# Dense gate and up of a two-layer transformer block with the weights as the stationary operand

## The reference

```python
def swiglu(h, wg, wu, wd):
    return (jax.nn.silu(h @ wg) * (h @ wu)) @ wd

for layer in range(DEPTH):
    h = h + hybrid_mixer(rms_norm(h, attn_norm[layer]), ...)
    hn = rms_norm(h, ffn_norm[layer])
    if layer % 2 == 0:
        h = h + swiglu(hn, dense_w_gate[j], dense_w_up[j], dense_w_down[j])
    else:
        h = h + moe_ffn(hn, moe_router[j], moe_w_gate[j], ...)
return rms_norm(h, final_norm)
```

## Time and profile before

| | before |
|---|---|
| median of 3 runs | 1602.93 us (1602.86 to 1602.99) |
| profiled execution, its own time | 1598.53 us |
| its span, first to last instruction | 1596.7 us |
| mean granted TensorE clock | 0.971 |
| TensorE matmuls busy | 1550.6 us (97%), 7086 of them |
| weight loads busy | 1252.5 us (78%) |
| DVE, ACT busy | 1266.9 us (79%), 1039.3 us (65%) |

### The profile page before, as it was taken

The page is one execution under the profiler, slowest core; times in us unless marked ns, Lnnn a source line. Parts: engine busy times, 40 slices in busy tenths (PEclk is TensorE's granted clock), DMA queues, the critical chain, the costliest instruction groups (busy, mean ns, idle before and its releaser), DMA issues.

```text
span 1596.7 us, 18779 instructions
## 1 busy us (share of the span) xinstructions
PE 1550.6 (97%) x7086; PEld 1252.5 (78%) x7086; DVE 1266.9 (79%) x1564; ACT 1039.3 (65%) x1328; POOL 58.7 (4%) x128
## 2 busy tenths in 40 slices
PE   7989999999899989999999999999999999999996
PEld 6867788888787778888888888888888888888885
DVE  6477655555548769899899899899899889999995
ACT  5444544443446457787788787787778778778774
POOL 2210000000113000000000000000000000000000
PEclk9978999999998789999999999999999999999998
DMA  7503454554252119999999999999999999999992
GB/s 282 191 2 106 177 197 172 182 187 160 86 180 106 54 67 372 373 359 360 341 358 365 334 357 370 343 354 368 337 364 356 343 358 362 345 369 362 358 359 95
DMA packets 181821, 431.61 MB, mean 270 GB/s; under 512 B 3808, under 2 KB 10336, under 8 KB 181728
## 3 DMA queue, kind: packets, MB, share of 16 engines
q1 hardware_dynamic: 180720, 428.01, 73.4%
q10 hardware_dynamic: 1008, 2.36, 0.4%
HBM read 429.31 MB, written 1.05 MB: 270 GB/s over the span
## 4 chain that ended last, share of the span: by engine, by line
PE 93%; DVE 4%; ACT 1%; issue 1%; POOL 0%; DMA 0%; DVEq 0%; SPq 0%; POOLq 0%
PE pair L828 50%; PE work L828 32%; PE pair L893 3%; PE work L804 2%; PE pair L804 2%; PE work L966 1%; PE work L815 1%; PE work L1069 1%; DVE arena L1519 0%; PE work L1083 0%; PE work L1084 0%; DMA h<-in_x 0%; DVE arena L1536 0%; DVE nmax L1550 0%; PE pair L896 0%
## 5 line engine op out<-in xcount | busy, mean ns | idle before, releaser
L1460 DVE TENSOR_TENSOR w_lo<-ring,w_hi 128x1024 fp32r<-128x1024 f32 (+3 forms) x810 | 967.1, 1215 | 198.5 <-ACT w_hi L1166 184.5
L1166 ACT ACTIVATE w_hi<-ring 128x1024 fp32r<-128x1024 f32 (+3 forms) x810 | 846.1, 1055 | 332.6 <-PE pair L828 177.2
L828 PE MATMUL pair<-w_hi,hnT_hi 128*128 128x512 f32 x672 | 269.2, 401 | 2.9 <-DVE hnT_lo L1468 2.6
L828 PE MATMUL pair<-w_hi,hnT_lo 128*128 128x512 f32 x672 | 265.9, 396 | 0.0
L828 PE MATMUL pair<-w_lo,hnT_hi 128*128 128x512 f32 x672 | 265.8, 396 | 0.0
L828 PE MATMUL work<-w_hi,hidT_hi 128*128 128x512 f32 x552 | 218.8, 396 | 2.6 <-DVE hidT_lo L1711 1.4
L828 PE MATMUL work<-w_lo,hidT_hi 128*128 128x512 f32 x552 | 218.1, 395 | 0.0
L828 PE MATMUL work<-w_hi,hidT_lo 128*128 128x512 f32 x552 | 218.1, 395 | 0.0
L828 PE MATMUL pair<-w_hi,xU_hi 128*128 128x512 f32 x448 | 179.4, 401 | 0.0
L828 PE MATMUL pair<-w_hi,xU_lo 128*128 128x512 f32 x448 | 177.0, 395 | 0.0
L828 PE MATMUL pair<-w_lo,xU_hi 128*128 128x512 f32 x448 | 176.9, 395 | 0.0
(11 more groups left out here) (205 smaller groups left out, 1373.9 us busy)
## 6 DMA issues: line engine op xcount, KB each, us to landing
ring<-in_moe_w_gate SPq DMA_DIRECT2D x56, 2048.0 KB, 9.2
ring<-in_moe_w_up SPq DMA_DIRECT2D x56, 2048.0 KB, 9.7
ring<-in_moe_w_down SPq DMA_DIRECT2D x56, 2048.0 KB, 8.9
ring<-in_dense_w_gate SPq DMA_DIRECT2D x7, 2048.0 KB, 7.8
ring<-in_dense_w_up SPq DMA_DIRECT2D x7, 2048.0 KB, 7.8
ring<-in_dense_w_down SPq DMA_DIRECT2D x7, 2048.0 KB, 8.0
ring<-in_w_in SPq DMA_DIRECT2D x4, 2048.0 KB, 9.5
ring<-in_w_out SPq DMA_DIRECT2D x4, 2048.0 KB, 9.4
```

The costliest lines, as they stand in the source:

```text
L828: mm = pe.matmul(b, lhs[x_part][k + kk], w[w_part][:, kk, :], start=(first and kk == 0 and i == 0), stop=(last and kk == 1 and i == 2))
L1166: return act.activation(o, i, ACT.Copy)
L1460: dve.tensor_tensor(lo, raw, hi.bitcast(F32), ALU.subtract).then_inc(lo_done, 1)
```

## The change

In turns 1 to 6, gate and up are made by a new `columns_turned`. The 128x128 tile of weights is stationary and the 256 tokens of both tiles move: for each part, block and column group of 128, 3 matmuls of 256 columns. The product has the hidden columns on the partitions, two column groups in each bank. Chunks 1 to 6 are not transposed any more; ACT and DVE split the hidden product out of `hid` in the same turn. The operands of odd chunks go into `y_hi` and `y_lo`, so that down of the chunk before can read `hidT_hi` and `hidT_lo` meanwhile. Chunk 0 stays as it was, transposed in turn 1. In the last turn down waits per bank for the additions of the turn before.

```diff
+        def dense_hidden(j):
+            if j % 2 == 0:
+                return hidT_hi[:, :, :, :], hidT_lo[:, :, :, :]
+            return [v[:, :].rearrange("p (t k s) -> p t k s", t=T, k=4) for v in (y_hi, y_lo)]
+        def of_columns(v, b):
+            return v.rearrange("p t k s -> p k t s")[:, 2 * b:2 * b + 2, :, :]
...
+            def columns_turned(part, banks):
+                for i in range(4):
+                    part_ready(part + i)
+                    w = part_buffers(part + i, 512)
+                    for kk in range(2):
+                        for f in range(4):
+                            b = banks[f // 2][:, f % 2 * S:f % 2 * S + S]
+                            for n, (x_part, w_part) in enumerate(((0, 0), (0, 1), (1, 0))):
+                                mm = pe.matmul(b, w[w_part][:, kk, f * P:(f + 1) * P], (hnT_hi, hnT_lo)[x_part][:, 2 * i + kk, :],
+                                               start=((i, kk, f % 2, n) == (0, 0, 0, 0)), stop=((i, kk, f % 2, n) == (3, 1, 1, 2)))
+                    mm.then_inc(part_used, 1)
...
                     elif j < NCH:
                         pe.wait_ge(silu_ready[0], T * j)
-                        columns(part, 0, hnT_parts, gate_bank)
+                        columns_turned(part, gate_bank)
                         part += 4
-                    if j:
-                        if 1 < j < NCH:
-                            pe.wait_ge(dense_added, 4 * (j - 1))
+                    if j == 1:
                         for t in range(T):
-                            turn(0, T * (j - 1) + t, t, dense_turn(j)[t])
-                    if j < NCH:
-                        if j:
-                            pe.wait_ge(hid_ready[0], T * j)
+                            turn(0, t, t, dense_down[1][t])
+                    if j == 0:
                         columns(part, 0, hnT_parts, up_bank)
                         part += 4
+                    elif j < NCH:
+                        pe.wait_ge(hid_ready[0], T * j)
+                        columns_turned(part, up_bank)
+                        part += 4
                     if j == NCH:
-                        pe.wait_ge(dense_added, 4 * (j - 1))
+                        pe.wait_ge(hidT_ready[0], T * j)
                         for t in range(T):
-                            pe.wait_ge(hidT_ready[0], T * (j - 1) + t + 1)
                             for i in range(4):
+                                if t == 0 and i % 2 == 0:
+                                    pe.wait_ge(dense_added, 4 * (j - 2) + 1 + i)
...
                     elif j:
+                        if j > 1:
+                            pe.wait_ge(dense_added, 4 * (j - 1))
                         pe.wait_ge(hidT_ready[0], T * j)
...
+            def hidden_high(j, b):
+                act.wait_ge(hid_ready[0], T * j + b + 1)
+                copy(of_columns(dense_hidden(j)[0], b), hid[:, b, :].rearrange("p (k t s) -> p k t s", k=2, t=T)) \
+                    .then_inc(hidT_hi_ready[0], 1)
...
-                        parts(11, 18 if j else 14)
+                        parts(11, 14)
+                    if 0 < j < NCH:
+                        for b in range(2):
+                            hidden_high(j, b)
+                        parts(15, 18)
...
+            def hidden_low(j, b):
+                dve.wait_ge(hidT_hi_ready[0], T * j + b + 1)
+                hi, lo = dense_hidden(j)
+                dve.tensor_tensor(of_columns(lo, b), hid[:, b, :].rearrange("p (k t s) -> p k t s", k=2, t=T),
+                                  of_columns(hi, b).bitcast(F32), ALU.subtract) \
+                    .then_inc(hidT_ready[0], 1)
...
-                    parts(14, 16 if j else 14)
+                    parts(14, 14)
+                    if 0 < j < NCH:
+                        for b in range(2):
+                            hidden_low(j, b)
+                        parts(15, 16)
```

More of the change, by code:

```diff
@@ L493, in places, with turned @@
             return found
-        def dense_turn(j):
-            return dense_down[1] if j < NCH else gate_bank
+        def turned(half, step):
+            return step + 1 - (DENSE_STEPS - T if half == 0 and step >= DENSE_STEPS else 0)
+        def dense_hidden(j):
[4 more added lines that the diff above has]
+            return v.rearrange("p t k s -> p k t s")[:, 2 * b:2 * b + 2, :, :]
         def first_step(half):
@@ L997, in _ @@
             hidT_parts = [[[v[:, t, k, :] for k in range(4)] for v in (hidT_hi, hidT_lo)] for t in range(T)]
+            dense_parts = [[[[v[:, t, k, :] for k in range(4)] for v in dense_hidden(j)] for t in range(T)] for j in range(2)]
             def dense():
@@ L1039, in dense @@
                                 part_ready(part + i)
-                                mm = part_product(part + i, 2 * (i % 2), hidT_parts[t], last_down[i // 2][t],
+                                mm = part_product(part + i, 2 * (i % 2), dense_parts[(j - 1) % 2][t], last_down[i // 2][t],
                                                   i % 2 == 0, i % 2 == 1)
@@ L1050, in dense @@
                             for t in range(T):
-                                mm = part_product(part, 2 * (i % 2), hidT_parts[t], dense_down[i // 2][t],
+                                mm = part_product(part, 2 * (i % 2), dense_parts[(j - 1) % 2][t], dense_down[i // 2][t],
                                                   i % 2 == 0, i % 2 == 1)
@@ L1304, in hidden_turned @@
             def hidden_turned(half, step, t, b):
-                act.wait_ge(tr_done[half], step + 1)
+                act.wait_ge(tr_done[half], turned(half, step))
                 copy(hidT_hi[:, t, :, :], b.rearrange("p (k s) -> p k s", k=4)).then_inc(hidT_hi_ready[half], 1)
+            def hidden_high(j, b):
+                act.wait_ge(hid_ready[0], T * j + b + 1)
+                copy(of_columns(dense_hidden(j)[0], b), hid[:, b, :].rearrange("p (k t s) -> p k t s", k=2, t=T)) \
+                    .then_inc(hidT_hi_ready[0], 1)
             def dense():
```

8 lines of the change are left out of this document (4 added, 4 removed).

## The result

| | before | after |
|---|---|---|
| median of 6 runs each | 1602.89 us (1597.79 to 1603.61) | 1591.99 us (1590.56 to 1595.15) |
| ratio, 95% interval | | 0.9948 (0.9933 to 0.9963) |
| profiled execution, and its span | 1598.53, 1596.7 us | 1595.15, 1593.3 us |
| its mean granted TensorE clock | 0.971 | 0.970 |

Repeated twice more with the same code it gave 0.9961 (0.9946 to 0.9977) and 0.9958 (0.9943 to 0.9974). Three of the six runs of before are the ones given ahead of the prediction; in the two repetitions the medians of before are 1599.03 and 1598.52 us.

The account below looks back on a forecast made before the run. The prediction took TensorE's matmul stream to bound the kernel, the dense stretch costing matmul count by distance of starts. Its terms, +3.7 - 4.4 - 2.3 = -2.9 us, took 1602.93 to 1600.0 us, range 1596.0 to 1604.0.

Parts of the forecast that it names:

- What bounds the kernel: Dense feed-forward of layer 0: TensorE is busy throughout, so time is the number of matmuls by the distance between their starts.
- Term 1: Gate and up of chunks 1 to 6: twelve products of 96 narrow matmuls at 0.120 us instead of 48 wide, +3.7 us.
- The lead of four short starts: Once per chunk, at gate behind 512-column matmuls, four starts come 0.005 us sooner each: 0.12 us less in all.
- Term 2: Transposes of chunks 1 to 5, between gate and up in turns 2 to 6, go: 0.88 us each turn, -4.4 us.
- Term 3: Last turn: the exposed transposes and TensorE's wait for ACT and DVE before down go, -2.27 us, moving layer 1's start.
- rival 2: Start of layer 1: other waits give back the 2.27 us saved in the last turn; -0.7 us net, 1602.3 us, chance 0.12.
- Term 4: ACT and DVE: the same copies and subtractions of the hidden product, now from SBUF, fit in idle time; 0 us.
- The sum: Whole change: +3.7 - 4.4 - 2.3 = -2.9 us, taking the profiled execution from 1598.53 to 1595.6 us.
- The base, 1602.93: Median of the runs before the change, 4.40 us above the profiled execution, from which 2.9 us was subtracted.
- The first: Rival on gate and up: narrow matmuls start every 0.1167 us, so they cost nothing extra; 1596.3 us, chance 0.14.
- Rival 3: New gate and up products: TensorE's instructions run short, ten packet fetches at 1.26 us, +9.7 net, 1612.6 us, chance 0.07.
- Rival 4: New products: loads stop running beside matmuls (0.188 us each, 1678 us) or the clock falls (about 1707 us); chance 0.03.

## Why the prediction was wrong, point by point

- **What bounds the kernel**: right. In this stretch the time is the number of matmuls by the distance of their starts; the experiments changed it by just that, but for the one whose added waits made TensorE stand and brought the clock down.
- **Term 1, +3.7 us: wrong, it measured +1.3.** The step that failed is "the trace has the same form elsewhere ... I take 0.120 us". Columns, type and loads were the same, and in all forms tried the gathering stays at 0.120 in a row of 48. But the pace goes with the distance of the two operands in memory, and between `hnT` and the weights it is 0.1178. The reading "the loads' pace, not the columns'" was wrong in its conclusion: with the same loads, the pace came out as 0.120, 0.1178 and 0.1167 with nothing changed but the operands' distance, and as 0.1133 in some products for a reason that is open. The lead of four short starts, 0.12 us, was not there either: the products take 11.31 behind wide matmuls and behind narrow ones.
- **Term 2, -4.4 us**: right, 4.44 by putting them back.
- **Term 3, -2.27 us**: right, 2.24. Layer 1's first product moved by the whole sum, counted from the start of the stretch, so rival 2 is out.
- **Term 4, 0**: right. The timeline of turn 6, ACT and DVE behind up (start, us, instruction):

```profile
388.73 1.29 DVE L1743 TENSOR_TENSOR arena<-pair,arena 128x512 f32<-128x512 f32 x2 [0.51 <-PE pair L1010]
389.70 1.14 ACT L1192 ACTIVATE hidT_hi<-arena 128x512 fp32r<-128x512 f32 x2
389.94 1.22 DVE L1496 TENSOR_TENSOR w_lo<-ring,w_hi 128x1024 fp32r<-128x1024 f32 x1
391.07 1.29 DVE L1754 TENSOR_TENSOR hidT_lo<-arena,hidT_hi 128x512 fp32r<-128x512 f32 x2
392.62 1.23 DVE L1496 TENSOR_TENSOR w_lo<-ring,w_hi 128x1024 fp32r<-128x1024 f32 x1 [0.27 <-ACT w_hi L1192]
```

  The two subtractions fill the gap that the earlier trace rows showed and leave 0.27 us idle. TensorE waits for neither.
- **The sum** -2.9 should have been -5.4. That would have been 1597.5 on the base that I took, inside my range. My -2.9 on the base named next would have been 1596.1, just inside as well: it took both errors, which went the same way. That the profiled execution, forecast at 1595.6, took 1595.15 is luck: the sum was 2.5 us too small, and its clock was 0.970 against 0.971 before.
- **The base, 1602.93: the second step that failed.** I added the sum to a median of three runs that stood 4.40 us over the profiled execution, and took this for a fixed offset. By their times these three were executions at the low end of the clock (0.968). From the median of before over 50 runs, 1598.96, the sum of -5.4 gives 1593.6; after measured 1591.99 in its own runs and 1592.4 over 21.
- **Rivals.** The first (1596.3) was the nearest: its mechanism, that narrow matmuls cost no more than their columns, is nearly so (0.1178) and exactly so with a shift of 32 bytes. Rival 3 (instructions run short): four packets more, all of them in the window of the earlier trace rows (11 instead of 7), and no wait for issue in the products. Rival 4: the clock stayed at 1.00 there and the loads stayed beside the matmuls, at a break-even of 0.1225. Its price for loads that do not overlap was too low: 0.188 us is the load alone, and with its 256 columns behind it a step would be some 0.30 us (an estimate: 0.188 + 0.1167).

## What to carry to other kernels

The pace of a matmul with its own weight load is not given by its form alone: before a pace is taken from another stage of the trace, look at where both operands lie, and price the change with both. A kernel that is all matmuls deserves a trial of a small unused buffer between the operands: here one line was worth 23 us, four times this change, and both together have the lowest median of all versions (1574.89 us, ratio 0.983), though its interval overlaps that of the shift alone. Only 32 and 128 bytes were tried. A base for a forecast of half a per cent needs the clock of the runs that it comes from, not only their median.

## What the hardware showed that I had not expected

- **The distance of operands changes the pace of float32r matmuls.** 256 columns, each with its own load of 128: 0.120 us in all pairs of operands that lie a multiple of 256 bytes apart; 0.1178 between `hnT` and the weights, 64 bytes short of a multiple; 0.1167 with 32 bytes more between them; 0.1134 or 0.1178 with 128 bytes more. 512 columns: 0.2333 at 64 and at 32 short, and 0.2290 with 128 bytes more, 64 over. Other distances were not tried. The Trainium skill (TensorE: Matmul & The Clock Gate, section Step-by-step: what each phase is for) says that the loads and the moving operand are read through two ports of their own, so that one does not take from the other. These runs don't show what is shared, but the time does depend on how the two operands lie to each other.
- **What ran before changes the pace of what follows.** Behind 12 to 48 added matmuls on `hnT` alone, the 96 of the next product took 10.88 us instead of 11.31 in some turns and not in others; the down product behind was at 11.19 to 11.20 again. Neither the number of added matmuls nor the turn being even or odd decides it.
- **Time follows the mean granted clock**, 1.24 us per 0.001 in a fit over this case's kernels; it fell in attention and routing (0.53 to 0.58 in the window 504 to 539, 0.87 in 560 to 600), and in the dense stretch only where an experiment made TensorE stand for some 4 us (0.79 to 0.98 in the product behind).
